# Waits for producers in place of stage barriers, the next norm inside the selection, and weighted slots for the first tile, in a one-core transformer layer

## What is computed

```python
h = LN(x) * (1 + scale1) + shift1
gq, gk, gv, glr, gog, sq, sk, sv, mg_a, mg_b = split_cols(h @ w_in)
o_gla, s_fin = gla_recurrence(q, k, v, log_a, s0)        # 4 heads, dk 128, dv 256
o_sb = stick_breaking(sbq, k_all, v_all, ...)            # 16 heads of 64, causal, cache of 1024
mix = (sigmoid(mg_a) * (o_gla @ w_gla_proj) + sigmoid(mg_b) * (o_sb @ w_sb_proj)) @ w_o
x  = LN1(alpha * x + gate1 * mix)
h2 = LN(x) * (1 + scale2) + shift2
# PEER: 8 heads, two top-16 of 128 keys, top 16 of their 256 sums
g = softmax(top); act = gelu(peer_u[eid] @ h2)
x  = LN2(alpha * x + gate2 * sum((g * act) * peer_v[eid]))
```

## Time and profile before

| | us |
|---|---|
| median of 3 runs (4528.18 to 4529.46) | 4528.57 |
| the profiled execution | 4524.86 |
| its span, first to last instruction | 4522.3 |
| TensorE busy (matmul) | 3384.7, 75% |
| VectorE busy | 2746.2, 61% |
| GpSimd busy | 2407.8, 53% |
| moved by DMA | 1572 MB, mean 348 GB/s |
| group 0's trunk, up to the last barrier | 0 to 964.7 |
| group 1's trunk | 964.7 to 2053.9 |
| group 2's trunk | 2053.9 to 3333.8 |
| the tail | 3333.8 to 4522.3 |

### The profile page before, as it was taken

One profiled execution on the slowest core, in us unless ns is written; L12 is line 12 of the kernel. 1 busy time (PEld: TensorE's weight loads), 2 busy tenths in 40 slices (PEclk: granted clock), 3 DMA queues, 4 the chain that ended last, 5 costly groups with the idle time before them and its releaser, 6 DMA issues.

```text
span 4522.3 us, 46382 instructions
## 1 busy us (share of the span) xinstructions
PE 3384.7 (75%) x16026; PEld 1667.0 (37%) x16026; DVE 2746.2 (61%) x6580; ACT 924.9 (20%) x1992; POOL 2407.8 (53%) x2375
## 2 busy tenths in 40 slices
PE   7988989878879989696899899798753433434355
PEld 4555755445536544253444356443320000000000
DVE  3343420689877864777776878655687676664420
ACT  3543210114432210013444523200100000000000
POOL 0000000134467756455877777655567777777776
PEclk9998999989989999898999999899865555555556
DMA  8774453478799999999999999999999999999998
GB/s 310 259 275 180 175 170 98 156 293 267 268 339 394 412 401 416 386 409 360 387 393 399 343 382 393 396 400 389 386 376 420 419 406 420 419 404 420 420 407 360
DMA packets 422694, 1572.17 MB, mean 348 GB/s; under 512 B 47720, under 2 KB 63464, under 8 KB 411328
## 3 DMA queue, kind: packets, MB, share of 16 engines
q0 software_dynamic: 340384, 1289.90, 72.6%
q1 hardware_dynamic: 78448, 271.38, 16.0%
q10 hardware_dynamic: 3632, 7.94, 0.5%
HBM read 1526.42 MB, written 42.61 MB: 347 GB/s over the span
## 4 chain that ended last, share of the span: by engine, by line
PE 44%; POOL 16%; DVE 16%; DMA 14%; issue 8%; ACT 2%; SPq 0%; ACTq 0%; DVEq 0%; POOLq 0%
PE wide L1847 8%; POOL peer_u_ring L2459 7%; DMA peer_v_ring<-in_peer_v,expertsT 6%; POOL peer_v_ring L2469 5%; PE bank L2526 5%; PE wide L2164 5%; DVE peer_u_ring L2632 4%; PE wide L1415 4%; POOL w_ring L2469 3%; PE wide L768 3%; DMA peer_u_ring<-in_peer_u,experts 3%; PE wide L1403 3%; PE bank L1847 2%; PE wide L831 2%; DMA w_ring<-in_peer_v,expertsT 2%
## 5 line engine op out<-in xcount | busy, mean ns | idle before, releaser
L2459 POOL DMA_INDIRECT peer_u_ring<-in_peer_u,experts x1098 | 1130.5, 1030 | 593.9 <-issue 287.5
L2632 DVE SCALAR_TENSOR_TENSOR peer_u_ring<-peer_u_ring,wide 128x1024 f32<-128x1024 f32 x682 | 821.3, 1217 | 560.1 <-DMA peer_u_ring<-in_peer_u,experts 541.7
L2469 POOL DMA_INDIRECT peer_v_ring<-in_peer_v,expertsT x840 | 880.6, 1048 | 478.1 <-PE bank L2526 254.5
L2526 PE MATMUL bank<-peer_v_ring,peer_lone 128*32 128x512 f32 x3360 | 559.4, 744 | 430.7 <-DMA peer_v_ring<-in_peer_v,expertsT 383.0
L2632 DVE SCALAR_TENSOR_TENSOR peer_u_ring<-peer_u_ring,peer_h 128x1024 f32<-128x1024 f32 x416 | 499.8, 1219 | 25.3 <-SPq L286 15.7
L2526 PE MATMUL bank<-w_ring,peer_lone 128*32 128x512 f32 x1056 | 249.9, 1035 | 348.1 <-DMA w_ring<-in_peer_v,expertsT 346.1
L2526 PEld LDWEIGHTS bank<-peer_v_ring,peer_lone 128*32 128x32 f32 x3360 | 78.2, 118 | 760.0 <-issue 712.9
L2469 POOL DMA_INDIRECT w_ring<-in_peer_v,expertsT x264 | 251.2, 951 | 84.4 <-issue 68.6
L2164 PE MATMUL wide<-mT,w_ring 128*128 128x384 f32 x768 | 266.3, 498 | 10.8 <-DMA w_ring<-in_weights 7.9
L768 PE MATMUL wide<-hT,w_ring 128*128 128x384 f32 x768 | 264.6, 491 | 6.1 <-DVE sb_hide L2746 3.1
L1415 PE MATMUL wide<-w_ring,hT 128*128 128x256 f32 x1152 | 263.8, 387 | 3.1 <-DVE gla_v L1741 3.1
(11 more groups left out here) (320 smaller groups left out, 5085.7 us busy)
## 6 DMA issues: line engine op xcount, KB each, us to landing
w_ring<-in_weights SPq DMA_DIRECT2D x312, 512.0 KB, 6.6
sb_kc<-in_kcT POOLq DMA_DIRECT2D x16, 2048.0 KB, 7.7
...
mod_w<-in_w_ada SPq DMA_DIRECT2D x15, 1024.0 KB, 11.1
...
mod_w_later<-in_w_ada SPq DMA_DIRECT2D x9, 1024.0 KB, 7.3
scores<-sel_sc SPq DMA_DIRECT2D x6, 1024.0 KB, 9.4
```

The costliest lines, as they stand in the source:

```text
L2459: pool.indirect_dma_start(buffer, None, K.A["peer_u"], bass.IndirectOffsetOnAxis(ap=K.ids_of[:, j % CHOSEN, k:k + 1], axis=0)).then_inc(lo ...
L2469: pool.indirect_dma_start(buffer, None, K.A["peer_v"], bass.IndirectOffsetOnAxis(ap=K.ids_of_turned[:, j % CHOSEN, t:t + 1], axis=0)).then ...
L2526: last = pe.matmul(self.F.psum[strip:strip + 32, :], self.lone[:, mark - at:mark - at + 32], self.buffer("v", m)[0][:, c * HALF:(c + 1) * ...
L2632: dve.scalar_tensor_tensor(u, u, 1.0, h2, ALU.mult, ALU.mult, accum_out=self.dots[:, j % 2, k:k + 1]).then_inc(self.dot_done, 1)
```

## The change

**Waits.** `stage_done` goes; only TensorE and VectorE still drain and add to a semaphore of their own at a stage's end (`ended`), and `after` waits for one or both of them where buffers are reused. Everything else waits for its producer: ScalarE in mix for the store of oA, in gla for the stores of k and v, in stick for the scores' stores; TensorE in res for each column of mT (`mix.added`) and each weight chunk as it comes; TensorE in select for ScalarE's last copies of h2; GpSimd's load of h2 for the stores of its rows. SyncE no longer waits for stores at a stage's end, but for TensorE's end of the stage before (for select, VectorE's too). TensorE's stick still waits for VectorE's norm in group 0.

**Mix order.** The first two columns' gate chunks come first (`MIX_ORDER`): four chunks that read hT, then four that read oA and oB.

**Norm.** The next group's rows are loaded to a buffer of their own at the start of the selection, and VectorE's part of the norm stands inside the selection, a piece behind each of heads 2 to 5. The exponentials of heads 6 and 7 move on ScalarE behind the norm's copies and into the attention.

**Paces.** The norm's two ticks cost 3 and not 10 in groups 1 and 2, and a slot of the first tile counts 0.8 when slots are dealt out. Slots done at the start of group 1's stick, gla, mix, res and select: 15, 168, 243, 311, 333 (before: 20, 157, 236, 308, 331); of group 2's: 372, 548, 624, 694, 716 (before: 378, 551, 626, 695, 717). Trunk's end: 754 in both. Dots in norm and select now read h2 from SBUF.

```diff
+LONE_U = 0.8
+MIX_ORDER = [(0, 0), (0, 1), (1, 0), (1, 1), (0, 2), (0, 3), (1, 2), (1, 3)] + [(j, m) for j in range(2, KC) for m in range(4)]
...
-    def start(self, e, G, name):
+    def after(self, e, G, name, *who):
 
         at = self.stage(G, name)
         if at:
-            e.wait_ge(self.stage_done, 4 * at)
+            for w in who:
+                e.wait_ge(self.ended[w], at)
...
-    def end(self, e):
-        e.drain().then_inc(self.stage_done, 1)
+    def end(self, e, who):
+        e.drain().then_inc(self.ended[who], 1)
...
-        units += [10.0] * 2
+        units += [3.0 if g.n else 10.0] * 2
...
-        total, done = sum(units[here:stop]), 0.0
+        weights = [LONE_U if s < SLOTS else 1.0 for s in range(before, to)]
+        total, done, at, spent = sum(units[here:stop]), 0.0, before, 0.0
         for w in units[here:stop]:
             done += w
-            out.append(int(before + (to - before) * done / total))
+            while at < to and spent + weights[at - before] <= sum(weights) * done / total + 1e-6:
+                spent += weights[at - before]
+                at += 1
+            out.append(at)
...
@@ Mix.tensor
-        K.start(pe, G, "mix")
-        for j in range(KC):
-            for m, x in enumerate((K.hT, K.hT, self.oA, self.oB)):
+        for c, (j, m) in enumerate(MIX_ORDER):
...
@@ Res.tensor
-        K.start(pe, G, "res")
-        w = [K.chunk(pe, G, RES_AT + n).rearrange("p (k n) -> p k n", k=2) for n in range(8)]
+        w = []
...
+                    if i == 0 and c == 0:
+                        pe.wait_ge(K.mix.added, KC * G.n + k + 1)
+                    if i == 0 and k % 2 == 0:
+                        w.append(K.chunk(pe, G, RES_AT + len(w)).rearrange("p (k n) -> p k n", k=2))
...
@@ Select.sync
-        K.start(sp, G, "select")
+        K.after(sp, G, "select", "PE", "DVE")
         sp.dma_start(self.keysT[:, :, :], K.A["keysT"]).then_inc(self.const_in, 16)
...
+        if G.n + 1 < len(GROUPS):
+            K.res.rows_stored(sp, G)
+            K.norm.load(sp, GROUPS[G.n + 1])
...
@@ Select.scalar
-            if h:
+            if 0 < h < PEER_HEADS - 1:
                 self.exp_best(act, G.first, h - 1)
...
@@ Select.vector
+        more = K.norm.scale_rows(dve, GROUPS[G.n + 1]) if G.n + 1 < len(GROUPS) else iter(())
...
+            if h >= 2:
+                next(more, None)
...
@@ Peer.by_banks
-        return self.K.dots_beside(s) not in ("stick", "gla")
+        return self.K.dots_beside(s) in ("mix", "res", None)
```

231 lines of the change are left out of this document (127 added, 104 removed).

## The result

The changed kernel takes **4503.76 us** (median of 4 runs, 4499.18 to 4504.82), beside 4529.01 (4 runs) for the kernel before on the same chip: ratio 0.9934, 95% interval 0.992 to 0.9948. It is 25 us faster where 64 were forecast, and lies 4 us above the range. The profiled execution has a span of 4501.7 us, against 4522.3.

The account below looks back on a forecast made before the run. Group 0 was taken as bound by its stages, group 1 to slot 128 by VectorE's stretch, then mostly by transfers (saturation 1.03). Gains 14 + 28 + 0 + 22 = 64 us gave 4464 us against the median 4528.57; range 4430 to 4500.

Parts of the forecast that it names:

- the exponentials: Selection, group 0 to 1: ScalarE reaches those of heads 6 and 7 before VectorE wants them; no term in the sum.
- group 2: Group 2's trunk: of 62 us lost at DMA share 0.98, a third regained, 22 us (0 to 40).
- Group 0: Group 0 up to its selection: barriers closed before gla, mix, res and select, 14 us gained (8 to 15).
- Slot 128: VectorE's first selection instruction to slot 128's dot: 28 us gained from fewer attention steps, barrier, waits and gaps (8 to 46).
- Behind slot 128: Rest of group 1 after slot 128, at DMA share 1.00: 0 us (5 lost to 15 gained).
- The price of 4 us: Group 1 after slot 128: traffic of four attention steps moved there, 1.8 MB or 4 us.
- Rival 1: Transfers keep all: group 2 bound by DMA, closed holes return as waits for peer_v; 38 us, 4490; chance 0.20.
- Rival 2: Stretch before slot 128 is a chain, waits for TensorE and ScalarE stay; 44 us, 4485; chance 0.13.
- Rival 5: After slot 128 TensorE's granted clock falls through many short waits; 96 us slower, 4625; chance 0.05.
- The rule of the Trainium skill: Dots in norm and select reading SBUF slow GpSimd's issues by contention: sum 50 us worse; forecast took 0.

Follow-up runs that it names:

- g1_exp: The kernel of e1_exp run again on a chip with a tail of 1188 us: ratio 0.9893, 4486.53 us.
- e3_even: The changed kernel with slots dealt out evenly (LONE_U 1.0 in place of 0.8): ratio 0.9967, 4677.54 us on a chip with a slow tail.
- f3_norm_end: The changed kernel with the norm's VectorE part behind the selection's last head again and all exponentials inside the selection: 4507.12 us, ratio 0.9934.
- e1_exp: The changed kernel with the exponentials of heads 6 and 7 back inside group 1's selection: ratio 0.9899, 4641.92 us on a chip with a slow tail.
- f1_point7: e1_exp with LONE_U 0.7 in place of 0.8: ratio 0.99, 4488.07 us.
- k2_holes: e1_exp with TensorE's waits at the stage ends put back in group 2 alone: ratio 0.9929.
- c_after: The changed kernel itself, run again as control: ratio 0.9938, 4507.24 us.
- k3_half: e1_exp with gathers of both tables cut to half rows beside group 2 (slots 378 to 759), those dots multiplied by zero: ratio 0.9818.

## Why the prediction was wrong

**The step that failed: the exponentials.** "Those of heads 6 and 7 ... both are reached near 957 and 969, before VectorE wants them." True in group 0, where they were reached at 946.96 and 960.14 and VectorE waited 0.2 us. The step was worked out for one of the two selections. In the other, TensorE's queue has pairs of peer_v in front of the transposes, and I had the row for it, TensorE's 104.3 us of waits for peer_v, but used it only as a loss to be regained. The sum has no term for it. Price: 28.3 us of VectorE's waits; 28.2 of the 39.5 us in the selection (177.0 against 148.8 in g1_exp); 21 to 27 us from slot 333 to 754; some 20 us of the whole time by the ratios. The other 11 us in the selection are the norm's own 9.4 us on VectorE, placed as forecast, and come back by slot 378 (162.9 us from slot 333, before 163.4). Without this step the time would have been 0.9893 of the kernel before, some 4480 us, inside the range.

**The second step: group 2.** "I expect a third of the loss to go: 22 us." With the exponentials in place, slots 333 to 754 take 1418.0 us against 1417.4 before. The term of 22 came to nothing, and that is about the other half of the miss. Why is open; what the runs rule out stands below.

**The sum, term by term.** Group 0: 14 forecast, 9.7 found. TensorE starts mix, res and selection 4.8, 8.7 and 10.2 us earlier, with idle times of 0.3 us before mix and res:

```profile
380.52 5.33 PE L1519 MATMUL wide<-hT,w_lr 128*16 128x384 f32 x16
...
611.55 18.66 PE L1878 MATMUL wide<-hT,w_ring 128*128 128x384 f32 x53 [0.26 <-issue]
...
778.50 21.70 PE L2030 MATMUL wide<-w_ring,mT 128*128 128x512 f32 x50 [0.26 <-issue]
...
845.63 12.60 PE L2203 MATMUL wide<-mT,w_ring 128*128 128x384 f32 x32 [3.09 <-DMA w_ring<-in_weights]
```

Gla starts without a wait, but no earlier than in the earlier trace rows, since the attention itself ended 2.5 us later in this run (it ended between 377.0 and 385.1 over all runs of the changed kernel and its variants). The selection waits 3.09 us for its first weight chunk. Slot 128: 28 forecast, 31.9 found. VectorE's work fell by 7.1 us (6.2 forecast), the barrier's 4.8 went, its waits in the attention fell from 27.0 to 8.4, by 18.6 (13.5 forecast), and the rest by 1.4 (4 forecast):

```profile
DVE sb_z L1212 <- PE wide L858: 6.9, 4, 3.0
...
DVE sb_l L1204 <- ACT sb_l L1077: 1.5, 3, 0.8
```

Alone, the 0.8 is worth 17 us there (e3_even) and the norm 8 (f3_norm_end), where I had given the norm 4.

**Behind slot 128.** 0 was right up to slot 333 (1.2). The price of 4 us that I had put on the 0.8 there, as transfers, is neither shown nor refuted: e3_even and e1_exp take the same time from slot 128 to 333, while f1_point7's 6 us are gone at slot 754. Group 2: 22 forecast; the 15.5 found from slot 370 on are the norm's work on the other side of the cut, and from slot 378 on it is 1254.0 before, 1255.0 after, 1255.1 in g1_exp. The reason behind the term was wrong. I took 1.03 as the DMA share of saturation and "a third of the loss" as what could be regained. But at 0.98 the bytes to be moved weren't the limit: two fifths less of them gave 2.4%. Nor is any other resource that was relieved alone: 83 us less of TensorE's work gave 17, 100 us less of VectorE's with 35 less of GpSimd's 13 to 16. That the engines go through one written order, in step through 14 buffers, so that each relief is used up at the next one, is the reading that fits these runs; no run shows it. More buffers in all, or fewer gathers, were not tried. The cause stays open in one more way: k2_holes puts the worth of the holes that the change closed at TensorE's stage ends behind slot 378 (some 20 us) at 10 to 16, and yet those slots take as long as before. Which part of the change gives this back wasn't found; part of it may be scatter, since the same stretch took 1246 and 1258 in f1_point7 and c_after, whose order there is the same.

**The rivals.** None had this mechanism. Rival 1 came closest: TensorE's waits for peer_v behind slot 128 went from 104.3 to 158.6 us, which was to be its sign, and with the exponentials in place its number fits too (38 us forecast, 36.4 found at slot 754 in g1_exp, waits for peer_v behind slot 378 up from 50.6 to 74.4). But its reason, that group 2 is bound by transfers, fell with k3_half; the number fits by luck. Rival 2 fell: VectorE's idle time before slot 128 halved. Rival 5 fell: the granted clock is 0.94 from slot 128 to 333 and in group 2, and 0.89 in the selection between them. The rule of the Trainium skill (GPSIMD Engine Reference, 1. Specifications) agrees in kind, 1193 against 948 ns for an issue of peer_v in the last selection, though those of peer_u took 953 and 963; it was worth some 3 us at most.

**The better version.** e1_exp and g1_exp, the change with the exponentials of group 1 left in the selection, stands at 0.9899 and 0.9893 of the kernel before, some 20 us better than the change; 0.7 for the slots or other paces in group 2 add nothing to it. It is still some 16 us short of the forecast.
